# One more group of stored activations, one more table turned in advance, and early stages cut by tiles in a two-block transformer kernel

## What is computed

```python
s = jnp.einsum('thpd,hpkd->thpk', q, subkeys)
s_top, i_top = lax.top_k(s, K)
cand = (s_top[:, :, 0, :, None] + s_top[:, :, 1, None, :]).reshape(t, PEER_HEADS, K * K)
c_top, c_idx = lax.top_k(cand, K)
e = i1 * N_KEYS + i2
g = jax.nn.softmax(c_top, axis=-1)
act = jax.nn.gelu(jnp.einsum('thkd,td->thk', ue, xb), approximate=False)
return jnp.einsum('thk,thkd->td', (g * act), ve)
```

## Time and profile before

| | us |
|---|---|
| median of 3 runs | 2684.51 (2682.45 to 2687.2) |
| the profiled execution's own time | 2692.68 |
| its span | 2690.9 |
| PE busy | 2444.7 (91%) |
| DVE busy | 1332.3 (50%) |
| ACT busy | 815.3 (30%) |
| POOL busy | 823.5 (31%) |
| mean granted clock of PE | 0.942 |

### The profile page before, as it was taken

How to read it: one execution, slowest core, us unless ns; L and a number is a source line. 1 busy time by engine, 2 the same in 40 slices (tenths; PEclk the granted TensorE clock), 3 DMA queues, 4 the chain that set the end, 5 groups by cost and what they waited for, 6 DMA issues and landing times.

```text
span 2690.9 us, 29210 instructions
## 1 busy us (share of the span) xinstructions
PE 2444.7 (91%) x11610; PEld 1234.5 (46%) x11813; DVE 1332.3 (50%) x2401; ACT 815.3 (30%) x873; POOL 823.5 (31%) x180
## 2 busy tenths in 40 slices
PE   6986498999989975898999969999999999999998
PEld 3465254444444443454456524444444444444443
DVE  1434553545442148278999655555555522222223
ACT  1212132333333233321148723322222223323221
POOL 0000022555555521131000124444443334244331
PEclk9955699999999986999999989999999999999999
DMA  5100011889886921021348876566666666666530
GB/s 192 63 32 0 31 63 49 246 240 252 240 248 191 255 69 39 32 95 51 145 184 317 316 225 187 172 192 183 191 187 188 169 204 172 173 187 167 145 93 39
DMA packets 399647, 418.64 MB, mean 156 GB/s; under 512 B 275243, under 2 KB 341935, under 8 KB 386869
## 3 DMA queue, kind: packets, MB, share of 16 engines
q1 hardware_dynamic: 393780, 406.69, 50.1%
q10 hardware_dynamic: 5760, 10.49, 1.1%
HBM read 280.82 MB, written 69.21 MB: 130 GB/s over the span
## 4 chain that ended last, share of the span: by engine, by line
PE 71%; DVE 19%; ACT 4%; DMA 2%; issue 2%; POOL 1%; SPq 1%; DVEq 0%; POOLq 0%; ACTq 0%
PE ps L1358 44%; PE ps L1587 10%; DVE arena L2221 4%; DVE arena L2228 4%; PE ps L1188 3%; PE ps L1627 2%; DMA gate_matrix<-split 2%; ACT split L1114 1%; PE ps L1186 1%; PE ps L1162 1%; ACT arena L1100 1%; PE ps L1603 1%; PE ps L1604 1%; PE ps L1259 1%; PE ps L1325 1%
## 5 line engine op out<-in xcount | busy, mean ns | idle before, releaser
L1358 PE MATMUL ps<-split,arena 128*128 128x512 bf16 x4421 | 982.0, 381 | 43.4 <-DVE x_sb L2243 14.5
L1358 PEld LDWEIGHTS ps<-split,arena 128*128 128x128 bf16 x4512 | 440.8, 98 | 580.4 <-issue 34.6
L787 POOL TENSOR_TENSOR split<-ring,split 128x4096 bf16<-128x4096 f32 x32 | 258.8, 8089 | 922.5 <-ACT split L1114 922.5
L1587 PE MATMUL ps<-arena 128*128 128x512 bf16 x1974 | 436.3, 379 | 2.2
L726 POOL TENSOR_TENSOR split<-ring,split 128x4096 bf16<-128x4096 f32 x31 | 246.9, 7966 | 413.4 <-ACT split L911 374.1
L1358 PE MATMUL ps<-arena,split 128*128 128x512 bf16 x1502 | 335.1, 380 | 14.1 <-DVE arena L1961 6.7
L2243 DVE TENSOR_TENSOR x_sb<-ps,x_sb 128x512 f32<-128x512 f32 x256 | 174.0, 689 | 337.3 <-PE ps L1358 337.3
L1587 PEld LDWEIGHTS ps<-arena 128*128 128x128 bf16 x2016 | 197.2, 98 | 237.9
L2221 DVE TENSOR_TENSOR arena<-arena 128x512 f32<-128x512 f32 x128 | 171.6, 1341 | 259.5 <-ACT arena L1107 170.5
L1358 PEld LDWEIGHTS ps<-arena,split 128*128 128x128 bf16 x1536 | 161.5, 106 | 181.9 <-issue 11.3
L2228 DVE TENSOR_TENSOR arena<-arena 128x512 bf16<-128x512 f32 x128 | 157.2, 1228 | 70.4 <-ACT arena L1109 36.7
(11 more groups left out here) (287 smaller groups left out, 2357.0 us busy)
## 6 DMA issues: line engine op xcount, KB each, us to landing
ring<-in_peer_v SPq DMA_DIRECT2D x32, 2048.0 KB, 7.5
ring<-in_peer_u SPq DMA_DIRECT2D x21, 2048.0 KB, 8.2
ring<-in_w_ff SPq DMA_DIRECT2D x16, 2048.0 KB, 8.2
gate_matrix<-split SPq DMA_DIRECT2D x16, 2048.0 KB, 8.1
arena<-gate_matrix SPq DMA_DIRECT2D x32, 1024.0 KB, 8.2
arena<-in_peer_u SPq DMA_DIRECT2D x44, 512.0 KB, 4.7
turned_table<-u_split SPq DMA_DIRECT2D x44, 512.0 KB, 5.4
ring<-turned_table SPq DMA_DIRECT2D x11, 2048.0 KB, 8.2
```

What stands on the lines that cost most here:

```text
L787: pool.tensor_tensor(split[:, s2, 1, :], ring[:, slot, :], split[:, s2, 0, :], ALU.subtract).then_inc(w_lo, 1)
L1358: mm = pe.matmul(dst, a(k), b(k), start=n == 0, stop=n == len(terms) - 1)
L1587: mm = pe.matmul(up_bank(j), a, b, start=n == 0, stop=n == len(terms) - 1)
```

## The change

`EARLY` becomes 11 and `PRE` 12. The early tiles are counted singly: 25 in the selection, 16 in the gate stage, and three behind it, ahead of the fresh group 11 and the first down. There are 48 units; chunks 15 to 18 get three each and the others two. In the last stage the rounds are eleven and the loop starts at group 22. In round 0 the high half of v(0) now stands between early tiles 41 and 42 on ACT; the halves of u(12) stand behind the fresh group's tiles (ACT) and behind v(1) (POOL); SP issues v(3), u(13), gates(3) and u(14) ahead of the transposes of u(12). The diff, cut to its core:

```diff
-        SORTED, EARLY, PRE = 6, 10, 11
+        SELECTED, GATED, EARLY, PRE = 25, 16, 11, 12
+        def pre_units(s):
+            if 3 <= s < 15:
+                return range(2 * s - 6, 2 * s - 4)
+            if 15 <= s < 19:
+                return range(3 * s - 21, 3 * s - 18)
+            return range(2 * s - 2, 2 * s) if 19 <= s < 25 else range(0)
...
-                if 4 <= m < 4 + 2 * PRE:
-                    n = 2 * (m - 4)
+                units = pre_units(m - 1)
+                for n in units:
                     pre_turn(n)
                     pre_load(n + 2)
-                    pre_turn(n + 1)
-                    pre_load(n + 3)
-                    pre_store(n)
-                    pre_store(n + 1)
+                    if n > units[0]:
+                        pre_store(n - 1)
+                if units:
+                    pre_store(units[-1])
...
+            sp.wait_ge(ex_a, 4 * 11)
+            load_u(12)
             for i in range(EARLY):
...
                 load_v(2 * i + 2)
+                if i == 0:
+                    sp.wait_ge(w_lo, S_EX + 2)
+                    load_v(3)
+                    sp.wait_ge(ex_a, 4 * g + 4)
+                    load_u(13)
+                    sp.wait_ge(ex_mul, 8)
+                    load_gates(3)
                 sp.wait_ge(u_split_lo, i + 1)
                 load_u(g + 3)
                 for half in range(2):
                     if i >= 1:
                         sp.wait_ge(ex_a, 4 * g + (2 * half + 2))
                     turn_rows(half)
...
             for s in range(15, 19):
                 split_low(s, s % 4)
-                for b in range(2):
-                    pre_low(2 * (s - 3) + b, b)
+                for n in pre_units(s):
+                    pre_low(n, n % 2)
...
-            for i in range(EARLY):
+            v_low(0, 0, 1)
+            v_low(1, 1, 0)
+            u_low(EARLY + 1, u_place(EARLY + 1)[0])
+            for i in range(1, EARLY):
                 v_low(2 * i, 0, 1)
                 u_low(EARLY + 1 + i, u_place(EARLY + 1 + i)[0])
                 v_low(2 * i + 1, 1, 0)
...
+            pre_high(13, 0)
+            def pre_chunk(s):
+                for n in pre_units(s):
+                    pre_high(n // 2, n % 2)
             split_high(16, 0, 5)
-            pre_highs(13)
+            pre_chunk(16)
             square_high(7, 1)
             split_high(17, 1, 5)
-            pre_highs(14)
+            pre_chunk(17)
             split_high(18, 2, 5)
-            pre_highs(15)
+            pre_chunk(18)
...
+            early_gelu(SELECTED + GATED)
             for q in range(2):
                 act.wait_ge(gate_stored[q], 16 * 8)
             for b in range(2):
                 act.wait_ge(pre_stored[b], 32 * PRE)
+            v_high(0, *v_place(0), 1)
+            for m in range(SELECTED + GATED + 1, 4 * EARLY):
+                early_gelu(m)
             for i in range(EARLY):
+                stored_tiles(2 * i)
                 if i == 0:
-                    v_high(0, *v_place(0), 1)
+                    v_high(1, *v_place(1), 0)
+                    live_tiles(EARLY, 1, None)
                     u_high(EARLY + 1, *u_place(EARLY + 1))
-                    stored_tiles(0)
...
-            for g in range(SORTED, EARLY):
+            for m in range(SELECTED, SELECTED + GATED):
+                up_begins(m // 4, m % 4)
...
+            for m in range(SELECTED + GATED, 4 * EARLY):
+                up_tile(m // 4, m % 4)
```

More of the change, by code:

```diff
@@ L613, in _ @@
                 load_turned(g)
-            for g in range(RING, EARLY):
+            for g in range(RING, 10):
                 sp.wait_ge(ex_a, 4 * (g - RING) + 4)
@@ L618, in _ @@
                 store_gates(n)
[L619 to L624, removed]
+                if n in (3, 7):
+                    g = 10 + n // 4
+                    sp.wait_ge(ex_a, 4 * (g - RING) + 4)
+                    load_turned(g)
                 if n == 11:
@@ L649, in _ @@
                     turn_rows(half)
[L650 to L656, removed]
+                if i >= 1:
+                    sp.wait_ge(w_lo, S_EX + 2 * i + 2)
+                    load_v(2 * i + 3)
+                    sp.wait_ge(ex_mul, 4 * (2 * i + 1) + 4)
+                    load_gates(2 * i + 3)
             for g in range(2 * EARLY, EX_GROUPS - 1):
[L658 removed]
+                sp.wait_ge(u_split_lo, g + 1 - EARLY)
                 if g + 3 < EX_GROUPS:
@@ L797, in _ @@
                 v_low(2 * i + 1, 1, 0)
[L798 to L802, removed]
+            with pool.Fori(0, 4) as i:
+                u_low(2 * i + 23, 3)
+                v_low(2 * i + 22, 0, 1)
+                u_low(2 * i + 24, 2)
+                v_low(2 * i + 23, 1, 0)
             u_low(31, 3)
@@ L1066, in _ @@
             act.wait_ge(w_used, 31)
[L1067 to L1073, removed]
-            act.sem_inc(gate_out, 2)
-            for g in range(SORTED, EARLY):
[L1076 to L1079, removed]
+            for m in range(SELECTED):
+                early_gelu(m)
+                if m == 17:
+                    act.wait_ge(gate_in, 1)
+                    act.activation(pick_g, pick_g, ACT.Exp).then_inc(gate_exp, 1)
+            act.sem_inc(gate_out, 2)
+            for m in range(SELECTED, SELECTED + GATED):
+                for n in range(4):
+                    gate_step(4 * (m - SELECTED) + n)
+                early_gelu(m)
             def u_high(g, slot, rounds):
@@ L1607, in _ @@
             pe.wait_ge(key_tops, 2 * P_HEADS)
[L1608 to L1616, removed]
-            pe.sem_inc(gate_mm, 4)
[L1620 to L1628, removed]
+            for m in range(SELECTED):
+                if m == SELECTED - 1:
+                    for i, src in enumerate((pick_1, pick_2, pick_g)):
+                        pe.wait_ge(picks_ready, i + 1)
+                        for t in range(NT):
+                            mm = pe.transpose(bank(i)[:, t * P:(t + 1) * P], src[:, t, :], ident)
+                        mm.then_inc(picks_turned, 1)
+                up_tile(m // 4, m % 4)
+            pe.sem_inc(gate_mm, 4)
+            for m in range(SELECTED, SELECTED + GATED):
+                up_begins(m // 4, m % 4)
+                terms = up_terms(m // 4, m % 4)
+                for q in range(4):
+                    gate_step(4 * (m - SELECTED) + q)
+                    for n in range(6 * q, 6 * q + 6):
+                        mm = pe.matmul(up_bank(m), *terms[n], start=n == 0, stop=n == len(terms) - 1)
+                mm.then_inc(ex_a, 1)
+            for m in range(SELECTED + GATED, 4 * EARLY):
+                up_tile(m // 4, m % 4)
             def expert_down(s, par, s2):
@@ L1650, in _ @@
                     expert_down(2 * i + 1, 1, 0)
[L1651 to L1655, removed]
+            with pe.Fori(0, 5) as i:
+                expert_up(2 * i + 22)
+                expert_down(2 * i + 21, 1, 0)
+                expert_up(2 * i + 23)
+                expert_down(2 * i + 22, 0, 1)
             expert_down(31, 1, 0)
@@ L2267, in _ @@
                 expert_add(2 * i)
[L2268 to L2272, removed]
+            with dve.Fori(0, 5) as i:
+                live_hidden(2 * i + 22, 2 * i + 22, 0, i * 16 + 192)
+                expert_add(2 * i + 21)
+                live_hidden(2 * i + 23, 2 * i + 23, 1, i * 16 + 192)
+                expert_add(2 * i + 22)
             expert_add(31)
```

26 lines of the change are left out of this document (13 added, 13 removed).

## The result

The changed kernel took 2699.31 us (median of 6 runs, 2692.56 to 2701.69), the kernel before, on the same chip, 2684.44 (6 runs, 2682.45 to 2687.99): 14.9 us slower by the medians. The forecast was +7.0 us, slower, with a range to 2703. Two executions further down, of 6579 us (experiment 7) and 8986 us (experiment 5), were slow ones and stand in none of the medians and ratios.

What follows compares the result with a forecast made beforehand. PE, with 71% of the chain, was taken as the bound, so time is won only where it waits. -3.7 - 24.1 + 1.0 + 33.8 = +7.0 us on 2684.5 gave 2691.5; own range 2678.5 to 2698, 8-in-10 range 2678 to 2703.

Steps and rivals of the forecast that it cites:

- The units: Feed-forward stage, chunks 15 to 18: four more units of rows, three a step, cost +33.8 us, bounds 21 to 40.
- The chain of a step: ACT, chunks 15 to 18: high half, low halves, transposes, issue, landing and high half follow in turn, 26.0 us a step.
- Its upper bound of 40: Top of the feed-forward term for the added units, with landings of 5.7 and 6.3 us adding 6.
- The rival with shorter transposes: Feed-forward stage: a transpose pair issues in some 2 us instead of 5.85; total -8.2 us, 2676.3; chance 0.07.
- The gate stage: Whole stage starts 1.45 us later and ends at 1527.1 on PE; its length changes by 0.
- The 25th tile: Selection: one more early tile ahead of the transposes, 5.18 us of work bought for 1.45 us: -3.7 us.
- The gap: Behind the gate stage, around the first down: PE loses 1.8 us instead of 25.9: -24.1 us.
- The additions: First down: DVE's additions start 8.1 us behind POOL's low half, at 1574.3; 1.8 us are lost.
- Hidden units: Rival, feed-forward stage: the added units stay hidden at a price of 0; 2657.7; chance 0.13.
- The fresh table of group 12 late: Rival, first round: half 0 lands late, 9 us of waiting and 2 of low clock; 2702.5; chance 0.12.
- The first down still waiting: Rival, behind the gate stage: DVE is held longer, half of the 24 us stays; 2703; chance 0.08.
- The signs named in the prediction: Feed-forward: sums end near 837, two PE waits of 15 to 20 us, four ACT load waits of 8 to 19.

Runs made afterwards that it cites:

- experiment 7: Changed kernel with three-unit steps spread over chunks 17, 19, 21 and 23, and 24 tiles in the selection instead of 25: 2664.77 us, ratio 0.9925.
- experiment 5: Changed kernel with three-unit steps at chunks 16, 19, 21 and 23, so one stands ahead of the squares: 2672.74 us, ratio 0.9956.
- Experiment 3: Changed kernel with SP issuing the load of unit n+2 ahead of unit n's two transposes, not behind them: 2692.88 us, ratio 1.0023.
- experiment 4: Changed kernel with its 48 units dealt otherwise, three at chunks 17, 19, 21 and 23, two elsewhere: 2661.61 us, ratio 0.9914.
- experiments 1 and 3: The first: changed kernel without the four extra units, group 11 using a copy of group 10's table, 2658.70 us, ratio 0.9896. The other: see Experiment 3.
- experiments 11 and 12: Kernel of experiment 4 with the gate stage's 2 MB loads cut into quarters: 2661.81 us with 25 selection tiles, 2662.99 us with 24.

## Why the prediction was right

The direction, the place and the mechanism held. Two terms of the sum were too small, by 4.7 and 3.8 us, and the measured +14.9 us is about twice the forecast. The result lies a little above the forecast's own range, 2678.5 to 2698. That the wider range to 2703 held it is in part luck: its top was set by two rivals that didn't happen.

**The units: +38.5 instead of +33.8.** The chain of a step was worked out as 26.0 us. Its ends, counted from chunk 15's high half:

| | forecast | measured |
|---|---|---|
| chunk 16's high half | 25.1 | 25.4 |
| behind unit 29, the first square | 51.5 | 52.1 |
| chunk 17's high half | 63.5 | 64.5 |
| behind unit 32, chunk 18's high half | 89.0 | 91.9 |
| behind unit 35, the sums | 115.1 | 119.6 |
| end of the sums | 119.9 | 124.4 |

The first two steps came within 0.6 us. The third took 27.4 us and the fourth 27.8, where the forecast had 25.5 and 26.1. Part of this is its arithmetic: the terms of a step add up to 26.0, and with the two waits for stores the steps would come out some 0.5 us longer each, 1.7 us in all. The rest shows in SP's timeline:

```profile
749.00 6.23 SPq L541 DMA_TRANSPOSE u_split<-u_split  x2
...
786.92 5.93 SPq L541 DMA_TRANSPOSE u_split<-u_split  x2
792.90 0.58 SPq L533 DMA_DIRECT2D arena<-in_peer_u  x1
793.60 5.54 SPq L541 DMA_TRANSPOSE u_split<-u_split  x2
...
814.84 8.00 SPq L541 DMA_TRANSPOSE u_split<-u_split  x2
```

The load issued at 792.90 let ACT go at 799.51, 6.6 us later, where the sum had 5.3 for issue and landing. In the fourth step the pair of transposes took 8.00 us, where the sum had 5.9. The term went by one pair and one landing where four of each were on the path. Its upper bound of 40 held the 38.5, but it counted longer landings only, and no longer pair. The rival with shorter transposes is out: the Trainium skill's 261 GB/s (DMA: Bandwidth & Descriptors, Latency and other measured facts), by which the whole change would have gained 9 us, is not what SP's rows show: SP stood 1.23 to 4.75 us over each 256 KB, 2.33 us in the median.

Experiment 3 corrects the picture behind the number. That the third unit's load stands behind the first unit's transposes is true, but taking it from there gives only 8.3 us, since the buffer of halves is the next holder. The prediction said that the waits "cannot be had earlier" in the program's order; with another order a part can, and by spreading the steps nearly all (experiment 4: 1.7 us left of 38.5).

**The gate stage: +3.8 instead of 0.** The prediction moved the stage by 1.45 us and took its length as it was. Its length hung on gate stores that stand behind 2 MB loads, with a longest wait of PE of 1.0 us before; in the changed kernel it was 2.1, and the clock and DVE followed. The rows for it (three waits of ACT for stores) were in the trace of before. With 25 tiles the stage took 145.6 and 145.7 us in experiments 1 and 3, where PE's longest wait for ACT was 1.4 us, and 148.1 or 148.2 in the others. The five profiles of some 148 us are those in which the granted clock fell to 0.50 for 3.4 us and DVE then waited 2.8 to 3.0 us at once, so that about 2.5 of the 3.8 us go with this fall. With 26 tiles, two waits of PE of 1.95 and 1.80 us without a fall went with 146.9 us. Why the stage falls the one way or the other isn't settled. That it hangs on the late stores is shown by experiments 11 and 12.

**Right.** The 25th tile costs 1.25 us of selection (1.45). The gap is gone, with 1.02 us of wait (1.8). The additions start 8.1 us behind POOL's low half, as taken. One row was read wrongly on the way: the 7.57 us in the earlier trace rows are DVE's low part (L2228), not its product, which took 4.90 us there beside POOL's low half of v(0), and takes 4.90 us in the changed kernel too. The times built on it held. That the additions follow POOL's end is because DVE is held once more; DVE's product and POOL's low half of v(1), from their timelines:

```profile
1592.19 7.98 DVE L2243 TENSOR_TENSOR arena<-arena 128x512 f32<-128x512 f32 x1 [3.30 <-ACT arena L1116]
```

```profile
1591.68 7.95 POOL L800 TENSOR_TENSOR split<-ring,split 128x4096 bf16<-128x4096 f32 x1 [10.97 <-ACT split L1132]
```

DVE's ends 0.54 us behind POOL's, while the product of the same shape at 1601.55 takes 0.69. This is what the Trainium skill says of the port that DVE and GpSimd share (SBUF — State Buffer, SBUF: two separate sides): whichever starts first has it for its whole instruction, and a DVE operation with two inputs in SBUF, as here, is held by it. POOL's started 0.51 us earlier, so the trace agrees.

**The rivals.** Hidden units: out, by four waits of ACT for rows. The fresh table of group 12 late: out, as no wait of PE stands between 1608.47 and the second fresh group at 1639.56. The first down still waiting: out, by the 1.02 us. The signs named in the prediction came too, if larger: ACT's four waits were 11.7 to 20.9 us (8 to 19), and PE's two 19.25 and 22.94 us (15 to 20).

## What to carry to other kernels

Where engines go through fixed lists with two buffers, cost a step as the chain through all its holders (load, halves, transposes, store), and then look at what stands behind its last member in each list: the same 26 us step cost 1.7 us once among shorter ones, 15.5 us ahead of the squares, and 38 us four times in a row. If the transfers of a stage have waiters, put an extra load between them in thin slices, one to a step. When a stage is moved by part of a step, look again at its small waits: one that is just covered may not be covered at its new place.

## What was not expected of the hardware

- A single wait of PE of 2.05 us in a stage in which it was otherwise busy (17.9 of the 20 us up to the end of the wait) was followed by a granted clock of 0.50 for 3.4 us, 0.91 as the mean of 20 us (the products of 128x128 behind it go from 0.22 to 0.31 us within half a microsecond). The same fall stands in five profiles, behind longest waits of 1.99 to 2.19 us. Longest waits of 1.0 and 1.4 us left the clock at 1.00, before and in experiments 1 and 3, and so did one of 1.95 us with 26 tiles. With figures so close the runs don't show whether the length of the wait alone decides.
- A pair of 256 KB transposes kept SP for 2.61 to 8.00 us in the chunks 15 to 18 (at 805.48 and 814.84), and how long went with what SP had issued ahead. All four pairs 2.1 to 3.3 us behind a weight load of 2 MB took 5.89 to 8.00 us, those right behind a load of rows 3.62 to 5.54, and those behind stores alone 2.61 to 2.84. In the other profiles with this order of SP's the three kinds keep apart nearly as well, with up to 10.4 us behind weight loads. No run varies this alone, so the cause isn't shown.
- The stages behind the gate stage repeat to 0.1 us over all kernels with the same number of tiles (1137.6 to 1137.8 with 25, 1141.6 to 1141.7 with 24), while those ahead of chunk 15 range from 706.0 to 718.7 us. So an effect of 3 us is plain in a stage and lost in a median.
